# The RWKV chunk inverse kept as its 32-position diagonal blocks, with the far block joined in a step of its own

## The reference

```
def step(S, inp):
    r_t, w_t, k_t, v_t, kk_t, a_t = inp
    sa = jnp.einsum('bhvk,bhk->bhv', S, -kk_t)
    S = (S * w_t[:, :, None, :] + sa[..., None] * (kk_t * a_t)[:, :, None, :]
         + v_t[..., None] * k_t[:, :, None, :])
    return S, jnp.einsum('bhvk,bhk->bhv', S, r_t)
```

## Time and profile before

| | before |
|---|---|
| median of 3 runs | 2879.13 us (2876.95 to 2888.28) |
| the profiled execution's own time | 2883.18 us |
| its span, first to last instruction | 2881.4 us |
| turns 1 to 6 of `rwkv_chunks`, from the first copy of turn 1 to that of turn 7 | 174.0 us, 29.0 us a turn |
| PE busy in a turn | 28.68 of 29.00 us |
| DVE, ACT busy in a turn | 17.07 and 9.01 us |
| mean granted TensorE clock of the span | 0.936; in the turns 1 to 6 it is 1.00 |

### The profile page before, as it was taken

How to read it: one execution, slowest core, us unless ns; L and a number is a source line. 1 busy time by engine, 2 the same in 40 slices (tenths; PEclk the granted TensorE clock), 3 DMA queues, 4 the chain that set the end, 5 groups by cost and what they waited for, 6 DMA issues and landing times. The chain is left out here.

```text
span 2881.4 us, 57941 instructions
## 1 busy us (share of the span) xinstructions
PE 2555.6 (89%) x20860; PEld 2090.6 (73%) x20860; DVE 1927.9 (67%) x2201; ACT 1603.9 (56%) x1867; POOL 379.6 (13%) x342
## 2 busy tenths in 40 slices
PE   5998899979989999999568999997597999999990
PEld 4776799847768888888457777776485788888870
DVE  3358356534479999999545666666335899999974
ACT  3656223253248888888324655554222788888861
POOL 0020000000013333333010000000000122222220
PEclk9999999989989999999779999998797999999995
DMA  3111000013269999999520111110323899999964
GB/s 95 45 44 30 27 4 4 4 60 127 88 231 377 385 382 383 382 375 378 198 72 26 36 38 37 32 31 9 141 75 123 329 376 376 382 383 387 381 256 188
DMA packets 219991, 525.39 MB, mean 182 GB/s; under 512 B 43824, under 2 KB 99120, under 8 KB 219824
## 3 DMA queue, kind: packets, MB, share of 16 engines
q1 hardware_dynamic: 201392, 489.34, 45.8%
q0 software_dynamic: 18432, 33.60, 3.1%
HBM read 506.06 MB, written 50.33 MB: 193 GB/s over the span
## 5 line engine op out<-in xcount | busy, mean ns | idle before, releaser
L1751 DVE TENSOR_TENSOR w_low<-w_raw,w_high 128x1024 fp32r<-128x1024 f32 x768 | 894.8, 1219 | 31.3 <-DVEq L52 21.7
L1464 ACT CAST w_high<-w_raw 128x1024 fp32r<-128x1024 f32 x768 | 755.1, 1049 | 109.1 <-ACTq L52 108.7
L1619 PE MATMUL ps<-w_high,x_high 128*128 128x512 f32 x1024 | 415.0, 405 | 7.5 <-PEq L52 6.6
L1623 PE MATMUL ps<-w_high,x_low 128*128 128x512 f32 x1024 | 404.0, 395 | 0.0
L1622 PE MATMUL ps<-w_low,x_high 128*128 128x512 f32 x1024 | 401.9, 393 | 0.0
L1619 PEld LDWEIGHTS ps<-w_high,x_high 128*128 128x128 f32 x1024 | 195.5, 191 | 50.6 <-issue 14.0
L1623 PEld LDWEIGHTS ps<-w_high,x_low 128*128 128x128 f32 x1024 | 194.2, 190 | 43.4
L2013 PE MATMUL ps<-h_high,w_high 128*128 128x512 f32 x512 | 213.4, 417 | 10.8 <-PEq L52 10.5
L1622 PEld LDWEIGHTS ps<-w_low,x_high 128*128 128x128 f32 x1024 | 195.0, 190 | 37.7
L1619 PE MATMUL ps<-w_high,hidden_high 128*128 128x512 f32 x512 | 200.7, 392 | 6.7 <-PEq L52 6.7
L2013 PE MATMUL ps<-h_high,w_low 128*128 128x512 f32 x512 | 201.9, 394 | 0.0
(11 more groups left out here) (402 smaller groups left out, 4865.6 us busy)
## 6 DMA issues: line engine op xcount, KB each, us to landing
w_raw<-in_moe_w_gate SPq DMA_DIRECT2D x256, 512.0 KB, 5.2
w_raw<-in_moe_w_up SPq DMA_DIRECT2D x256, 512.0 KB, 5.6
w_raw<-in_moe_w_down SPq DMA_DIRECT2D x256, 512.0 KB
w_raw<-expert_rows SPq DMA_DIRECT2D x32, 512.0 KB, 9.1
w_tiles<-in_c_w_in SPq DMA_DIRECT2D x32, 512.0 KB, 4.0
w_tiles<-in_ab_w_in SPq DMA_DIRECT2D x22, 512.0 KB, 3.9
residual<-in_x SPq DMA_DIRECT2D x16, 512.0 KB, 7.3
h_rows<-hn_moe SPq DMA_DIRECT2D x16, 512.0 KB, 2.9
```

Of the source, the lines that this page charges most:

```text
L1464: act.copy(wh[:, p, :], raw[:, p, :]).then_inc(high_made, 1)
L1619: ins = pe.matmul(ps[:, bank, :], high, w_h, start=first, stop=False)
L1623: return pe.matmul(ps[:, bank, :], low, w_h, start=False, stop=final)
L1751: dve.tensor_tensor(wl[:, p, :], raw[:, p, :], wh[:, p, :].bitcast(F32), ALU.subtract).then_inc(low_made, 1)
```

## The change

The inverse is no longer kept as one 64x64 matrix for each head and chunk, but as its two diagonal blocks of 32x32. The tile XX holds X and its transpose, each as 32 columns on all 128 partitions: four blocks (2 heads x 2 blocks of positions) on four groups of 32 partitions. So:

- `t1` and `dx` have four levels instead of five. Each now has 32 products (before 16) of 32x32 for `t1`, and 64 (before 32) for `dx`, at four diagonal places of the array.
- `gram_b` computes L and its transpose only inside the 32-blocks (`near`: 8 products of 64 rows x 32 columns for each n), the block of L that joins the two (`far`, 2 products), and the r-b matrix as before (2 products of 64x64). ScalarE copies them as `near_out`, `far_copy`, `rb_copy`.
- The last level becomes `t1_far` (16 products of 32x32) and `dx_far` (32 products), which give YT, the 32 columns of the transposed inverse that belong to the second block, copied by `y_far_out`.
- `sa` multiplies in two parts: the first 32 rows with XX (32x32 weights, 64 columns), the second 32 rows with YT (64x32 weights, 64 columns), alternately for each head pair.
- The tiles that VectorE and ScalarE handle have 256 elements on a partition instead of 512 in `level`, `t1_out` and the start of X; `x_add` takes X and XT in one addition for each group.
- `ds(f - 1, 0)` is moved ahead of `t1(f, 2)`, and `gram_b(f + 1, 0)` behind it.
- GpSimd makes the masks for 32-blocks on four groups of partitions instead of two.

```diff
+                for p in range(0, P, BD):
+                    low = c.lower_1[p:p + BD, :].rearrange("p (n h) -> p n h", h=2)
+                    keep(low, [[-2, BD // 2], [-1000, 2]], -1, 1)
+                    keep(low, [[2, BD // 2], [0, 2]], 1, -1)
+                    for i, w in enumerate(LEVELS[:-1]):
+                        up = c.upper[p:p + BD, i, :].rearrange("p (n h q) -> p n h q", h=2, q=w)
+                        keep(up, [[-2 * w, BD // (2 * w)], [1000, 2], [0, w]], -1000, 1)
+                        keep(up, [[2 * w, BD // (2 * w)], [0, 2], [0, w]], w - 1, -1)
...
-    NLV = len(LEVELS) - 1
+
+    BD = 32
+    NLV = len(LEVELS) - 2
...
+        near = ps[:, 2, :].rearrange("p (m i n) -> p m i n", m=2, n=BD)
+        rb = ps[:, 0, :].rearrange("p (i n) -> p i n", n=HD)
+        far = ps[:, 1, 0:NI * BD].rearrange("p (i n) -> p i n", n=BD)
+        t1_ps = ps[:, 3, 0:NI * BD].rearrange("p (i n) -> p i n", n=BD)
+        far_ps = ps[:, 4, 0:NI * BD].rearrange("p (i n) -> p i n", n=BD)
+        dx_ps = lambda g: ps[:, 4 + g, 0:NI * BD].rearrange("p (m i n) -> p m i n", m=2, n=BD)
+
+        blocks = [(h, q, bl, slice(h * HD + bl * BD, h * HD + (bl + 1) * BD)) for h, q in halves for bl in range(2)]
+        first, second = ([rw for _, _, bl, rw in blocks if bl == i] for i in range(2))
...
                 def gram_b(f, ci):
-                    pe.wait_ge(tok_ready, 3 * f + 2 + ci)
-                    tk = chunk(f, ci)
+                    pe.wait_ge(tok_ready, 3 * f + 3)
                     for j in range(NPAIR):
                         n = ci * NPAIR + j
-                        for mv, to in ((ab, gram[:, n, 0, :]), (r, gram[:, n, 1, :])):
-                            for h, q in halves:
-                                pe.matmul(to[q], bb[q, j, tk], mv[q, j, tk], start=True, stop=True)
+                        for m, (left, right) in enumerate(((bb, ab), (ab, bb))):
+                            for h, q, bl, rw in blocks:
+                                at = block_of(f, ci, bl)
+                                pe.matmul(near[rw, m, n, :], left[q, j, at], right[q, j, at], start=True, stop=True)
+                        for (h, q), rw in zip(halves, first):
+                            pe.matmul(far[rw, n, :], bb[q, j, block_of(f, ci, 0)], ab[q, j, block_of(f, ci, 1)], start=True, stop=True)
                         for h, q in halves:
-                            last = pe.matmul(low[q, n], ab[q, j, tk], bb[q, j, tk], start=True, stop=True)
+                            last = pe.matmul(rb[q, n, :], bb[q, j, chunk(f, ci)], r[q, j, chunk(f, ci)], start=True, stop=True)
                     last.then_inc(lt_done, 1)
...
                 def t1(f, lv):
                     pe.wait_ge(lo_done, NLV * f + lv + 1)
-                    if lv == 0:
-                        pe.wait_ge(x_first, f + 1)
+                    for n in range(NI):
+                        if lv and n % NPAIR == 0:
+                            pe.wait_ge(x_next, 2 * (NLV * f + lv) - 1 + n // NPAIR)
+                        for h, q, bl, rw in blocks:
+                            last = pe.matmul(t1_ps[rw, n, :], LO[rw, lv, n, :], XX[rw, f % 3, 0, n, :], start=True, stop=True)
+                    last.then_inc(t1_done, 1)
+
+                def dx(f, lv):
+                    pe.wait_ge(t1_copied, (NLV + 1) * f + lv + 1)
                     for g in range(2):
-                        if lv:
-                            pe.wait_ge(x_next, 2 * (NLV * f + lv) - 1 + g)
-                        for j in range(NPAIR):
-                            for h, q in halves:
-                                n = g * NPAIR + j
-                                last = pe.matmul(t1_at(g)[q, js(j)], LO[q, lv, n, :], X[q, f % 2, n, :], start=True, stop=True)
+                        for i in range(NPAIR):
+                            n = g * NPAIR + i
+                            for h, q, bl, rw in blocks:
+                                pe.matmul(dx_ps(g)[rw, 0, i, :], XX[rw, f % 3, 1, n, :], T1[rw, n, :], start=True, stop=True)
+                                last = pe.matmul(dx_ps(g)[rw, 1, i, :], T1[rw, n, :], XX[rw, f % 3, 1, n, :], start=True, stop=True)
+                        last.then_inc(dx_done, 1)
+
+                def t1_far(f):
+                    pe.wait_ge(far_out, f + 1)
+                    for n in range(NI):
+                        if n % NPAIR == 0:
+                            pe.wait_ge(x_next, 2 * NLV * (f + 1) - 1 + n // NPAIR)
+                        for r0, r1 in zip(first, second):
+                            last = pe.matmul(t1_ps[r1, n, :], FAR[r0, f % 2, n, :], XX[r0, f % 3, 0, n, :], start=True, stop=True)
                     last.then_inc(t1_done, 1)
 
-                def dx(f, lv):
-                    pe.wait_ge(t1_copied, NLV * f + lv + 1)
-                    for g in range(2):
-                        for j in range(NPAIR):
-                            for h, q in halves:
-                                n = g * NPAIR + j
-                                if lv < NLV - 1:
-                                    pe.matmul(dx_at(g, 0)[q, js(j)], XT[q, f % 3, n, :], T1[q, n, :], start=True, stop=True)
-                                last = pe.matmul(dx_at(g, 1)[q, js(j)], T1[q, n, :], XT[q, f % 3, n, :], start=True, stop=True)
-                        last.then_inc(dx_done, 1)
+                def dx_far(f):
+                    pe.wait_ge(t1_copied, (NLV + 1) * (f + 1))
+                    for n in range(NI):
+                        for r0, r1 in zip(first, second):
+                            pe.matmul(far_ps[r0, n, :], T1[r1, n, :], XX[r1, f % 3, 1, n, :], start=True, stop=True)
+                            last = pe.matmul(far_ps[r1, n, :], c.ident[r1, r1], XX[r1, f % 3, 1, n, :], start=True, stop=True)
+                    last.then_inc(y_far_done, 1)
...
                 def sa(f, ci):
                     pe.wait_ge(u_copied, 2 * f + ci + 1)
-                    pe.wait_ge(x_next, 2 * NLV * (f + 1) - 1 + ci)
+                    pe.wait_ge(y_far, f + 1)
                     if f or ci:
                         pe.wait_ge(y_copied, 2 * f + ci)
                     for j in range(NPAIR):
-                        for h, q in halves:
-                            last = pe.matmul(o_sa[q, js(j)], XT[q, f % 3, ci * NPAIR + j, :], U[q, ci, j, :], start=True, stop=True)
+                        n = ci * NPAIR + j
+                        for r0 in first:
+                            pe.matmul(o_sa[r0, js(j)], XX[r0, f % 3, 1, n, :], U[r0, ci, j, :], start=True, stop=True)
+                        for (h, q), r1 in zip(halves, second):
+                            last = pe.matmul(o_sa[r1, js(j)], YT[q, f % 3, n, :], U[q, ci, j, :], start=True, stop=True)
                     last.then_inc(sa_done, 1)
...
                     dx(f, 1)
+                    if seq:
+                        ds(f - 1, 0)
+                    if not nxt:
+                        head_sum(3)
+                    t1(f, 2)
                     if nxt:
                         gram_b(f + 1, 0)
                     else:
-                        head_sum(3)
-                    t1(f, 2)
-                    if seq:
-                        ds(f - 1, 0)
+                        head_sum(4)
                     dx(f, 2)
                     if nxt:
                         gram_b(f + 1, 1)
                     else:
-                        head_sum(4)
                         head_sum(5)
                     t1(f, 3)
...
-                    t1(f, 4)
+                    t1_far(f)
...
-                    dx(f, 4)
+                    dx_far(f)
...
+                def near_out(f):
+                    act.wait_ge(lt_done, 2 * f + 2)
+                    if f >= 2:
+                        act.wait_ge(lo_done, NLV * (f - 1))
+                    act.copy(LT[:, f % 2].rearrange("p m i n -> p (m i n)"), ps[:, 2, :]).then_inc(lt_out, 1)
+
+                def far_copy(f):
+                    act.wait_ge(lt_done, 2 * f + 2)
+                    act.copy(FAR[:, f % 2].rearrange("p i n -> p (i n)"), ps[:, 1, 0:NI * BD]).then_inc(far_out, 1)
+
+                def rb_copy(f):
+                    act.wait_ge(lt_done, 2 * f + 2)
                     if f >= 2:
                         act.wait_ge(masks_done, f - 1)
-                    act.copy(LT[:, f % 2, ci * NPAIR:(ci + 1) * NPAIR].rearrange("p i m n -> p (i m n)"), ps[:, ci, :]).then_inc(lt_out, 1)
-
-                def low_copy(f):
-                    act.wait_ge(lt_done, 2 * f + 2)
-                    if f:
-                        act.wait_ge(x_first, f)
-                    act.copy(LW[:].rearrange("p i n -> p (i n)"), ps[:, 2, :]).then_inc(low_out, 1)
+                    act.copy(RW[:, f % 2].rearrange("p i n -> p (i n)"), ps[:, 0, :]).then_inc(rb_out, 1)
...
                 def x_start(f):
-                    dve.wait_ge(low_out, f + 1)
```

(50 more changed lines are left out.)

64 lines of the change are left out of this document (33 added, 31 removed).

## The result

| | before | changed |
|---|---|---|
| median, us (4 runs each) | 2880.4 (2876.95 to 2888.28) | 2990.73 (2985.37 to 2992.46) |
| ratio | | 1.0376, 95% interval 1.036 to 1.0391: slower |
| profiled execution, its span | 2883.18, 2881.4 | 2989.53, 2987.8 |
| granted clock, mean over the span | 0.936 | 0.919 |

A forecast was written before the change was run, and what follows sets the result against it. PE was taken as the bound, by number of passes times their pace. Six middle turns +9.6, turn 0 -5, turn 7 -2, ahead +1.5, behind +2 gave +6 us: 2889 profiled, median 2885, range 2835 to 2940.

The forecast's parts named there:

- the sum of a middle turn: Turns 1 to 6: -15.9+1.9+1.0+8.2+6.1+0.3 = +1.6 us each, +9.6 for six.
- the number of passes times their pace: Six turns cost this, since every copy and addition lies behind other products; 29.2 ns a pass before.
- Pace of four places: Narrow passes on four array places: 8.5 ns each, 960 of them +8.2 us a middle turn.
- Changes of shape: Switching tile shape on PE: 0.13 us each, 47 in a middle turn, +6.1 us.
- the stretch of 1.79 us in the earlier trace: Evidence that 128x64 to 128x32 places also pays: said to be 0.12 us longer than its passes explain.
- The rival of two places at a time: Four places run only two at a time, 16.2 ns a pass: 2943 us; chance 0.16.
- The rival of 29.2 ns whatever the columns: Every pass costs 29.2 ns: +22 us a turn, about 3050 us; chance 0.04.
- The Trainium skill's floor: Start-to-start never below about 25 ns: 1024 passes take 25.6 us, an estimated 16 more a turn; prediction rejected it.
- The clock: Granted clock at 1.00 (2.4 GHz) in the turns; leaving it because of gaps would make the forecast wrong.
- Ends: Outside the six middle turns: turn 0 -5 us, turn 7 -2, ahead of turn 0 +1.5, behind turn 7 +2.

The follow-up runs named there:

- e7: Changed kernel with parts of t1 and dx in hardware loops from turn 1 on: as many passes executed, 384 fewer delivered a turn; 2953.82 us.
- e5: Kernel before, with products of t1 and dx computing only 32 of their 64 columns from turn 1 on; 2884.64 us.
- e2: Changed kernel with the products of dx at level 0 written out and issued five times instead of once; 3102.64 us.
- e3: Changed kernel with dx at level 0 executed five times, the four extra times as a hardware loop around one written copy; 3032.82 us.
- e10: Kernel before with three satisfied waits ahead of products of t1, ds and gram_k, except the first of each step; 2930.62 us.
- e11: Kernel before with three satisfied waits ahead of products of all nine functions of a turn; 3133.18 us.

## Why the prediction was wrong

- **The step that failed** is the sum of a middle turn, and under it the sentence that six turns cost the number of passes times their pace. It priced each pass by the array and left out that its two instructions must be delivered. 1504 x 27.0 ns = 40.6 us against the 30.6 forecast: 10 of the 12.7 us a turn that were missing. I had read the narrow stretches of the earlier trace rows, 32 and 64 passes long; a run that short can come out of one packet, and the limit only shows over several. In the kernel before, the passes take 29.2 ns, just over the 27.0, so "number of passes times their pace" held there.
- **Pace of four places**: 8.9 ns in `t1` for 8.5 forecast. In `dx` it is 11.6 (32 passes in 0.37 us): 512 x 3.1 = 1.6 us a turn too little. With it the forecast's turn is 32.2, and e7 shows 32.5. So even nearly without the limit the turn is 1.9 us over the forecast; 0.8 us of that are waits by issue that e7's turn still has.
- **Changes of shape**: 0.12 in `sa`, 0.13 forecast. Right, and nearly without effect, since the time passes into the wait for the next packet. One of its readings was off: the stretch of 1.79 us in the earlier trace rows is 0.10 us longer than the prediction's own sum of 1.69, and not 0.12.
- **The rival of two places at a time** had 0.16 and stood at 2943, 48 us below the result. It is wrong: at 32 columns the passes of `t1`, whose four places write one bank, follow each other by 8.9 ns and those of `dx` by 11.6, where it needs 16.2.
- **The rival of 29.2 ns whatever the columns** had 0.04 and stood at 3050, 59 us above. Its mechanism is wrong for the new tiles and right for the old ones (28.8 ns with 32 columns in e5).
- **The Trainium skill's floor** of 25 ns, in TensorE: Matmul & The Clock Gate, "Wait — 56ns, not 53.3ns?", gave a turn 16 us over the prediction's sum; 12.7 came. That it is near is luck: the trace does not agree with it as a floor between two matmuls, which stand 8.9 ns apart, and the 27.0 ns hold only on average over a packet.
- **The clock** left 1.00, which the prediction named as a way to be wrong. In e7 turns at 0.87 are 3.4 to 3.9 us longer than the one at 1.00. In the changed kernel six turns exceed six times 40.6 by 16 us. They took 70 packets, so 3.7 us each in place of 3.45. Packets of 64x64 passes need that long at 29.2 ns, some packets came later, and the clock took its part; the shares are not separated. Why the clock falls is not settled: e7 has hardly a wait by issue, and its later turns lose clock too.
- **Ends**: turn 0 was forecast -5 and is +8.7: its 1216 passes or so meet the same limit, 32.8 us. Ahead of it +2.9 against +1.5, behind turn 6 +9.2 against 0.

What the runs show: delivery decides (e2 against e3, and e7 in the other direction), at 3.45 us a packet at best at either clock, and in the stretches that wait, the next transfer begins only about 1.1 us after TensorE has begun on the last packet. Why the next packet is not fetched earlier stays open, and no run changed the size of a packet.

The Trainium skill, in Runtime: NRT & Kernel Launch, "Instruction fetch mechanics", says that instructions come in blocks of 16 KiB, 256 of them, and that crossing a block is mostly hidden. The blocks agree with the 12 packets of 0.20 MB. Hidden it is in the kernel before; in the changed one it is the bound.

No version here beats the kernel before. As an estimate, a turn with the 960 passes of before, however fast in the array, could win at most 29.0 - 25.9 = 3.1 us; no run tried it on smaller tiles.

## What to carry to other kernels

Count TensorE's instructions beside its array time: in this unrolled code a weight load and a matmul together needed at least 27 ns on average, so splitting a product into more and smaller ones gains nothing once a pass is cheaper than that, and each pass added cost 27 ns (e2). Read it in the trace by idle times ended by issue at equal distances, with equal counts between them, and by the packets of the instruction queue. A hardware loop around a body with fixed addresses escapes it, at 0.12 to 0.36 us a taken branch in e7.

## What was unexpected of the hardware

- TensorE gets one packet of 256 instructions per 3.45 us or so at best, at granted clocks of 0.50 and 1.00 alike, though the transfer takes only 0.95 us of it.
- A pass on a 64x64 tile takes 29 ns with 32 or 64 moving columns; on 32x32 tiles at four places 8.9 to 11.6.
- Three satisfied waits ahead of a product, one of them an instruction of its own, cost TensorE 48 to 70 ns (e10, e11).
